# First attention stage of a two-block transformer kernel: norm after the projections, early logits, forget biases in one pass, another order of loads and turns

## The reference

```python
def rmsnorm(x, g):
    xf = x.astype(jnp.float32)
    y = xf * lax.rsqrt(jnp.mean(xf * xf, axis=-1, keepdims=True) + RMS_EPS)
    return (y * g.astype(jnp.float32)).astype(x.dtype)

def fox_attention(q, k, v, log_f):
    c = jnp.cumsum(log_f, axis=-1)
    ...
        sc = (jnp.einsum('bhqd,bhkd->bhqk', qb, k, preferred_element_type=jnp.float32) * scale
              + cb[..., :, None] - c[..., None, :])
        p = masked_softmax(sc, kpos[None, :] <= qpos[:, None])
        return jnp.einsum('bhqk,bhkd->bhqd', p.astype(v.dtype), v)

def even_mixer(h, w_in, b_f, ...):
    (fq, fk, fv, f_logit, nq, kc, vc, ks, vs, kw, vw, g_logit) = jnp.split(h @ w_in, EVEN_SPLIT_IDX, axis=-1)
    log_f = jax.nn.log_sigmoid(f_logit.astype(jnp.float32) + b_f.astype(jnp.float32)).transpose(0, 2, 1)
    o_fox = fox_attention(to_heads(fq, H_FOX), to_heads(fk, H_FOX), to_heads(fv, H_FOX), log_f)
    ...
```

## Time and profile before

| | us |
|---|---|
| median of 3 runs | 2014.54 |
| lowest, highest | 2012.95, 2021.45 |
| span of the profiled execution | 2011.9 |
| busy in it: PE, PEld, DVE, ACT, POOL | 1953.4, 1727.1, 1340.9, 1010.4, 320.4 |

### The profile page before, as it was taken

How to read it: one execution, slowest core, us unless ns; L and a number is a source line. 1 busy time by engine, 2 the same in 40 slices (tenths; PEclk the granted TensorE clock), 3 DMA queues, 4 the chain that set the end, 5 groups by cost and what they waited for, 6 DMA issues and landing times.

```text
span 2011.9 us, 34435 instructions
## 1 busy us (share of the span) xinstructions
PE 1953.4 (97%) x12338; PEld 1727.1 (86%) x12338; DVE 1340.9 (67%) x2732; ACT 1010.4 (50%) x1640; POOL 320.4 (16%) x138
## 2 busy tenths in 40 slices
PE   7998999999999999999999999999999999999998
PEld 6776787778778888999899999999999998888886
DVE  6357556656655558889787689933667766666666
ACT  5436546555554456666444455665444443333333
POOL 0000000000000000000000057877666600000000
PEclk9899999999989999999999999999999999999999
DMA  6242465533345553444343535555444455555554
GB/s 229 74 157 78 157 205 167 178 121 128 118 137 188 187 188 126 147 138 136 105 126 126 179 126 168 180 175 167 137 142 142 137 164 188 192 193 192 193 193 156
DMA packets 85150, 313.99 MB, mean 156 GB/s; under 512 B 9456, under 2 KB 9456, under 8 KB 84592
## 3 DMA queue, kind: packets, MB, share of 16 engines
q1 hardware_dynamic: 85040, 312.49, 46.6%
HBM read 311.40 MB, written 1.05 MB: 155 GB/s over the span
## 4 chain that ended last, share of the span: by engine, by line
issue 61%; PE 32%; POOL 6%; DVE 0%; POOLq 0%; DVEq 0%; ACT 0%
PE ps L414 17%; PE ps L282 12%; POOL wsplit L266 6%; PE ps L2642 3%; PE ps L430 0%; DVE work L2772 0%; DVE sq L2679 0%; POOLq L265 0%; PE ps L2718 0%; POOLq L2505 0%; DVE sq L2675 0%; DVE picks L2595 0%; PE ps L2608 0%; DVEq L2930 0%; DVE work L2687 0%
## 5 line engine op out<-in xcount | busy, mean ns | idle before, releaser
L260 ACT ACTIVATE wsplit<-ring 128x1024 fp32r<-128x1024 f32 x572 | 603.8, 1057 | 475.4 <-PE ps L414 270.4
L266 DVE TENSOR_TENSOR wsplit<-ring,wsplit 128x1024 fp32r<-128x1024 f32 x438 | 534.6, 1223 | 326.1 <-ACT wsplit L260 324.7
L282 PE MATMUL ps<-hsplit,wsplit 128*128 128x256 f32 x5064 | 646.2, 287 | 6.5 <-DVE hsplit L698 2.1
L282 PEld LDWEIGHTS ps<-hsplit,wsplit 128*128 128x128 f32 x5064 | 620.3, 193 | 14.3 <-issue 5.2
L266 POOL TENSOR_TENSOR wsplit<-ring,wsplit 128x1024 fp32r<-128x1024 f32 x134 | 320.2, 2396 | 1295.5 <-ACT wsplit L260 1295.5
L414 PE MATMUL ps<-wsplit,gsplit 128*128 128x512 f32 x1992 | 458.1, 391 | 0.0
L414 PEld LDWEIGHTS ps<-wsplit,gsplit 128*128 128x128 f32 x1992 | 374.4, 188 | 81.9 <-issue 4.2
L401 PE MATMUL ps<-wsplit,hsplit 128*128 128x512 f32 x1248 | 310.0, 406 | 17.2 <-DVE wsplit L266 10.6
L401 PEld LDWEIGHTS ps<-wsplit,hsplit 128*128 128x128 f32 x1248 | 241.9, 196 | 70.4 <-issue 18.9
L1783 PE MATMUL ps<-hsplit,wsplit 128*128 128x256 f32 x936 | 128.5, 289 | 0.0
L1783 PEld LDWEIGHTS ps<-hsplit,wsplit 128*128 128x128 f32 x936 | 116.3, 191 | 0.0
(11 more groups left out here) (318 smaller groups left out, 1698.5 us busy)
## 6 DMA issues: line engine op xcount, KB each, us to landing
ring<-in_weights SPq DMA_DIRECT2D x580, 512.0 KB, 3.3
work<-in_tables SPq DMA_DIRECT2D x1, 2123.0 KB, 12.5
xT<-in_x SPq DMA_DIRECT2D x1, 1024.0 KB, 4.9
work<-in_subkeys SPq DMA_DIRECT2D x1, 1024.0 KB, 15.2
work<-in_decay SPq DMA_DIRECT2D x2, 512.0 KB, 4.1
out_x<-work SPq DMA_DIRECT2D x2, 512.0 KB, 2.6
work<-in_w SPq DMA_DIRECT2D x1, 512.0 KB, 5.9
ring<-in_gain_row SPq DMA_DIRECT2D x1, 512.0 KB, 3.8
```

What stands on the lines that cost most here:

```text
L260: act.activation(wsplit[:, n % RING, 0, :], slab(s), ACT.Copy).then_inc(S("split", "lead"), 1)
L266: eng.tensor_tensor(wsplit[:, n % RING, 1, :], slab(s), wsplit[:, n % RING, 0, :], ALU.subtract).then_inc(S("split", RESTS[stream][0]), 1)
L282: mm = pe.matmul(dst, wsplit[:, n, a, c * P:(c + 1) * P], hsplit[:, b, c, :], start=(c == 0 and t == 0), stop=(c == KC - 1 and t == 2))
```

## The change

- **Norm.** `hT`, L385 and the second split (m0) are gone. Queries and keys are projected from the n0 split, and `rinv` is multiplied in when they are copied out of PSUM: one DVE operation of 128x512 for each turn (`fox_query_key_vector`) in place of two ACT copies. The fox and nsa values are scaled by token when they are copied out; for nsa, `rinv` is put into its own cosine and sine tables once.
- **Logits.** Forget and gate weights are one group of 56 columns, multiplied by the gains once (DVE, 128x448). `logits_tensor` runs them straight from `xT` after the second quarter of the values, 16 matmuls, each k twice: to PSUM partitions 0 to 63 and 64 to 127. The gate logits are turned by two small transposes.
- **Sum of squares.** GpSimd adds the eight chunks of squares down to two (`fold_gpsimd`, three operations of 128x512); TensorE then needs two matmuls, not eight.
- **Biases.** The running sum has its rows in four copies in each half of the partitions. It is split into a leading and a low part (one-pass type), and the bias matmul has 64 rows of the one-pass type (L824). The key side is made for each turn, two DVE operations. A turn's four score matmuls come first, then its four bias matmuls.
- **Turns.** Queries of odd and even turns have banks of their own, so a query waits for the copy of two turns before. TensorE turns the probabilities of turn u-1 ahead of the scores of u, and makes the values of u-1 after the key of u+1. ACT takes one slab lead before and one after the turned copy.
- **Loads.** Gains first, x in halves, two slabs, `small`, the third slab, the first 1940 of 4248 columns of tables. Masks and subkeys are loaded behind the nsa slabs, the other tables in the first feed-forward.
- The semaphores of the HGRN and Hyena stages are merged (`in`, `staged`), with the same instructions around them.

```diff
     def fox_tensor(pe, st, pre):
         for q in range(4):
             mm = split_columns(pe, st, q, q, 4, pre=pre)
-            if q == 0:
-                norm_tensor(pe, pre, 7)
-            if q == 2:
-                column_tensor(pe, pre, 7)
+            if q == 1:
+                logits_tensor(pe, st)
+                folded_norm_tensor(pe, 7)
         mm.then_inc(S("pair", "v"), 1)
...
         fox_query_tensor(pe, 0)
+        column_tensor(pe, pre, 7)
         fox_key_tensor(pe, 0)
-        gate_logits_tensor(pe, st)
         pe.wait_ge(S("load", "made"), 3)
+        gate_turn_tensor(pe, st)
         pe.wait_ge(S("pair", "v_sb"), 1)
         for u in range(4):
             if u < 3:
                 fox_query_tensor(pe, u + 1)
+            if u:
+                fox_probs_tensor(pe, u - 1)
             pe.wait_ge(*pair("qk_sb", u))
-            pe.wait_ge(S(st, "bias_steps"), 2 + min(u, 1))
+            pe.wait_ge(S(st, "bias_steps"), u + 3)
...
             scores_tensor(pe, qk_turn[:, 0, :], qk_turn[:, 1, :], 3, u).then_inc(S("pair", "scores"), 1)
             if u < 3:
                 fox_key_tensor(pe, u + 1)
             if u:
-                fox_probs_tensor(pe, u - 1)
                 fox_values_tensor(pe, u - 1)
...
+    def logits_tensor(pe, st):
...
+        for k in range(KC):
+            for hh in range(2):
+                mm = pe.matmul(ps[HD * hh:HD * hh + HD, 6, 0:T], strided(small_("wfg"), k * N_WFG, [[1, HD]]), xT[:, k, :],
+                               start=(k == 0), stop=(k == KC - 1))
...
+    def fox_query_key_vector(v, u):
+        v.wait_ge(*pair("qk", u))
+        v.tensor_tensor(qk_turn[:, :, :], ps[:, u % 2, :].rearrange("p (a t) -> p a t", a=2), rr[:, :, :],
+                        ALU.mult).then_inc(S("pair", "qk_sb"), 1)
...
+        if bias is not None:
+            for hh in range(2):
+                for tt, c0, keys in SEGS:
+                    h_ = slice(HD * hh, HD * hh + HD)
+                    mm = pe.matmul(ps[:, bank0 + hh, c0:c0 + keys], bias_q[h_, tt * P:(tt + 1) * P],
+                                   bias_k(bias, hh)[:, 0:keys], start=False, stop=True, skip_group_check=True)
...
-        load(xT[:, :, :], x, "x")
+        load(gains_sb[:, :], gains, "gains")
+        for half in range(2):
+            load(xT[:, 4 * half:4 * half + 4, :], x[:, 4 * half:4 * half + 4, :], f"x{half}")
+        load_slab(0, weights[0])
+        load_slab(1, weights[1])
         load(sm, small, "small")
...
```

More of the change, by code:

```diff
@@ L124, in end, with build @@
         assert self.i is None or self.n == self.per + self.base, (self.n, self.per)
-def build(nc, weights, small, tables, masks, w3, decay, subkeys, gain_row, x, out):
+def build(nc, weights, small, gains, tables, masks, w3, decay, subkeys, gain_row, x, out):
     ctx = ExitStack()
@@ L2808, in stream @@
                 load_slab(s, weights[s])
-        load(xT[:, :, :], x, "x")
-        load(sm, small, "small")
-        for s in range(RING):
-            load_slab(s, weights[s])
-        load(tab, tables, "tables")
-        load(level_masks, masks, "late")
-        load(sub, subkeys, "late")
+        load(gains_sb[:, :], gains, "gains")
+        for half in range(2):
+            load(xT[:, 4 * half:4 * half + 4, :], x[:, 4 * half:4 * half + 4, :], f"x{half}")
+        load_slab(0, weights[0])
+        load_slab(1, weights[1])
+        load(sm, small, "small")
+        load_slab(2, weights[2])
+        load(tab[:, 0:FIRST_TABLES], tables[:, 0:FIRST_TABLES], "tables")
         at = RING
@@ L2834, in _ @@
                         at += 1
+                    load(level_masks, masks, "late")
+                    load(sub, subkeys, "late")
                     continue
@@ L2879, in _ @@
         act.preload_act_table(ACT.Sqrt)
-        act.wait_ge(S("load", "made"), 2)
+        act.wait_ge(S("load", "made"), 1)
+        act.wait_ge(S("load", "gains"), 16)
         fox_scalar(act, "fox")
@@ L3115, in pack @@
     return {
-        "weights": weights, "small": small, "tables": tables, "masks": masks,
+        "weights": weights, "small": small, "gains": gs.reshape(11, KC, P).transpose(2, 0, 1).reshape(P, -1), "tables": tables, "masks": masks,
         "w3": f("filt_w3_2")[0], "decay": f("filt_decay_2"),
```

254 lines of the change are left out of this document (137 added, 117 removed).

## The result

| | before | after |
|---|---|---|
| median, us | 2013.98 (4 runs) | 1991.7 (4 runs, 1990.87 to 1992.53) |
| span of the profiled execution | 2011.9 | 1989.1 |
| first matmul | 10.59 | 10.95 |
| first scores | 44.36 | 42.57 |
| first projection of nsa | 89.41 | 67.64 |

The ratio is 0.9881, 95% interval 0.9864 to 0.9897. Forecast were 1995.7 us and a range of 1990.5 to 2005.0. A reader should know that the kernel before scatters: beside the later experiments it took 2012.46 to 2022.2 us, with granted clocks of 0.979 to 0.988, while the changed kernel stayed within 1.7 us. The trace of before that the prediction was read from is one of its best executions.

What follows compares the result with a forecast made beforehand. TensorE, busy 97% of the span, was taken as the bound. Front 2.5, turns 17.0 and behind them 0.8 sum to 20.3 us; one clock fall leaves 18.8, so 2014.5 - 18.8 = 1995.7 us, range 1990.5 to 2005.

Steps and rivals of the forecast that it cites:

- the added wait: Front: TensorE, done with key and gates at 36.1, waits 2.7 us for DVE's rest of slab 6.
- one fall of the clock: Behind the added wait: the clock falls once, costing 1.5 us (a projection 4.63 instead of 3.13).
- The start: First lead no longer waits for `small`, 430 KB less ahead, worth 1.1 us; TensorE starts at about 9.5.
- The front's sizes: First 24 matmuls 5.3 plus 2.9 us; sixteen logits matmuls 4.6 us, with 3.7 and 7.4 kept as bounds.
- A turn's scores: Each turn: scores 0.92 us (from nsa's row without biases) plus four biases 0.7, so 1.6 (1.4 to 3.0).
- The turns' projections: From first scores to nsa: five projections at 3.13 us each, 15.7 in all.
- my 28.1: TensorE's time from first scores to nsa, one wait included, against 45.05 before: 17.0 us won.
- The one wait: Turn 3, which has no query: probabilities of turn 2 come late by 1.1 us.
- My cross-check: The turns' 17.0 us won, split: scores 10.6, clock 3.0, waits 2.3, the rest the last turn's slow clock.
- Behind the turns: From nsa on: 0.8 us more won by clock; masks and subkeys delay no slab before 180 us.
- Better than that: Rival: no fall of the clock, logits pairs at 3.7, scores at 1.4; 22.0 us won, 1992.5 us; chance 0.10.
- bound by the chain of engines: Rival: turns wait for probabilities or moved transfers interfere; 6 us go, 12.8 won, 2001.7 us; chance 0.13 (chain or transfers).

Runs made afterwards that it cites:

- Experiment 7: Kernel after with slab 0 loaded between the two halves of x; 1989.13 us, ratio 0.9853.
- experiment 12: Kernel after with the logits' two halves one behind the other (eight chunks to partitions 0 to 63, then eight to 64 to 127); 1996.51 us.
- experiment 3: Kernel after with each bias matmul right behind its score matmul, still one-pass with 64 rows; 1992.68 us.
- experiment 4: Kernel after with the bias matmuls in full precision f32, 64 rows kept; 1995.46 us.
- Experiment 10: Kernel after with TensorE's old order in the turns: probabilities of turn u-1 turned behind the key of u+1; 1997.04 us, ratio 0.9903.
- experiment 6: Kernel after with masks and subkeys loaded ahead of the last nsa slab; 1992.26 us, ratio 0.9868.
- experiment 1: Kernel before without the sixteen bias matmuls of the four turns; 1995.94 us, ratio 0.9885.
- experiment 2: Kernel before with a turn's four score matmuls first and its four bias matmuls (full precision, 16 rows) behind them; 2000.29 us.
- experiment 8: Kernel after with slab 6's rest ahead of the column, masks and subkeys ahead of the last nsa slab, slab 0 between x's halves; 1988.83 us.
- experiment 11: Kernel after without GpSimd's additions of the squares: eight matmuls with ones in place of two; 1994.22 us.
- experiment 5: Kernel after with DVE's rest of slab 6 put ahead of the copy of the column; 1990.61 us, ratio 0.9858.

## Why the prediction was right and wrong

The direction and the mechanism held: the gain is in the turns, TensorE stayed the bound behind them, the added wait stood where I put it (2.85 us, forecast 2.7, at 38.04), with one fall of the clock behind it (1.5 us forecast, 4.60 - 3.1 measured). The size was short by 4.0 us of span. Along the trace, after was ahead of the forecast by 3.9 us at nsa's first projection, 3.5 at its third, 1.7 at L667, 2.5 at 1632 us and 4.0 at the end. So the error lies ahead of nsa, 3.0 us of it in the turns; a loss and a gain behind them nearly cancel, and the last 1.5 us are luck as far as the runs show. By my steps:

- **The start: wrong sign.** Forecast 9.5, measured 10.95. I counted bytes ahead of the lead, but the first ACT step waited for x until 6.09 and the lead for slab 0 until 8.54, behind the second half of x. Experiment 7 shows 9.35 with slab 0 ahead of it. That is not the whole cause: before, slab 0 lay behind all of x and `small` and was there for its lead at 8.18. From 2 to 4 us the queue moved 299 GB/s then and 206 in after; why was not tried (the 44 KB of gains now go first). Cost 1.45 us in this trace.
- **The front's sizes.** The first 24 matmuls took 7.3 us, not 8.2. The logits took 3.67 and not 4.6: the lower bound, full overlap, was the right end (experiment 12: 6.31 without). With the start these cancel: first scores at 42.57, forecast 43.4 with the clock counted. The 7.3 us are partly luck, since the same 24 matmuls took 7.0 to 8.5 in the eight kernels with this order of loads.
- **A turn's scores: the step that failed.** I took 1.6 us (bounds 1.4 to 3.0), 0.92 for the four scores and 0.7 for the four biases; it is 1.05, 2.2 us less in four turns and below my lower bound. The scores take 0.68 us up to the start of the biases, because the 0.92 of my row is a duration up to the modelled end of the last one. The biases take 0.37 up to the next projection. My lower bound of 0.5 priced all four at 256 columns, but two have 128 (one behind the other, at a projection's price, that would be 0.38), and the two halves of the rows run side by side: the single records of after show the biases starting in pairs, at 43.249 and 43.262 us, then at 43.449 and 43.465. I had used this overlap for the scores, whose row contains it, and not for the biases; how much is due to the columns and how much to the overlap is not shown. Experiments 3 and 4 size it: 0.5 us a turn for alternation, 0.56 for the type.
- **The turns' projections.** I summed durations (five of 3.13); starts lie closer, 14.9 us for five and not 15.7, since one row's end overlaps the next row's start. Together with the scores this is the 3.0 us between my 28.1 and 25.07. The one wait was right (1.1 forecast, 1.17 measured).
- **What won them.** My cross-check gave 10.6 us to the scores, 3.0 to the clock and 2.3 to the waits. By the runs the grouping alone is 12.0 of the 20.0 us (7.2 in the eight matmuls, most of the rest in the clock), 64 rows in two halves 3.0 (four turns of 0.75), the one-pass type 2.4, and some 2.5 are left for the order of turns, the queries' own banks and the copies on DVE together, which fits 3.45 us of waits becoming 1.17. These last shares are differences between single executions of unlike kernels, an estimate. Experiment 10 gives TensorE's order 5.2, but with a mismatch of its own.
- **Behind the turns: wrong.** I wrote that the masks and subkeys delay no slab before 180 us. TensorE waited 1.02 us at 171.84, and experiment 6 takes this wait away. Of 22.3 us at the third nsa projection, 20.5 are left at L667. The first two nsa projections gave 0.5 us from start to start (0.8 by their durations), forecast 0.8.
- **The second block: not forecast, and not shown to be the change's.** 1.5 us come at its last part. The product behind HGRN ran there at a granted clock of 0.96 before (46.6 us from 1653.41) and at 1.00 after, with seven more matmuls begun in the same time. Experiments 1 and 2 show 0.96 too, which looks like something that another part of the change mends. But of the eleven kernels with the change two also show 0.96 there and take the 1.5 us longer, experiments 8 and 11. First experiment 8, then after:

```profile
1629.15:1675.73 46.58, 46.58 (x198) 37.88 (x199) 30.65 (x52) 16.97 (x16) 0.00 (x0) 0.96 0.56 180
```

```profile
1632.12:1678.70 46.58, 46.58 (x205) 38.06 (x206) 31.42 (x53) 18.04 (x17) 0.00 (x0) 1.00 0.56 184
```

So a single execution of the changed kernel has this fall of the clock or has it not; whether the change makes it rarer (two of eleven, against three of three) stays open. Without these 1.5 us the profiled span would have been 2.5 us under the forecast and not 4.0.

Of the rivals none came as told. "Better than that" was nearest (1992.5) but wanted the clock not to fall; it fell as counted, and the gain came from the scores and the projections of the turns instead. The turns were not bound by the chain of engines in after; in experiments 5 and 8, which shorten the front, they became so.

The Trainium skill, page "TensorE: Matmul & The Clock Gate", section "HAM oscillation — how this bites in real kernels", has the clock fall at waits between bursts. The traces agree in part: it fell behind the wait of 2.85 us in after and behind 1.66 us in experiment 8, but not behind 1.65 us in experiment 5, nor behind the same 2.85 us in experiment 3 (in the seven other kernels with that wait it fell each time, 4.43 to 4.61 us for the projection); and before it fell at 59.62 with no wait over 0.9 us, where grouping the scores kept it up (experiment 2) with the same waits. In the one execution of each, matmuls that alternate between 64 and 16 rows did more to the clock of the turns than the waits: without the alternation (experiments 1 and 2) it stayed at full speed.

## What to carry to other kernels

Price small matmuls by how neighbours in the list relate, not one by one: put those of one shape and type together, and let neighbours use different halves of the rows or of the output partitions. When a front gets shorter, look at once at the slowest follower's queue (here DVE's) and move what nobody needs yet behind the first thing that is now waited for; otherwise the time comes back as a wait two steps on, with a fall of the clock on top. Order the first loads by first use in pieces, since half of x ahead of the first weights cost some 1.1 us here. And size an edit by the stage that it touches, not by the span of one execution.

## What the runs showed of the hardware that I had not expected

- Scores and biases alternating between 64 and 16 rows cost 4.16 us for eight full-precision matmuls, the same eight grouped 2.36 us, and the granted clock of the turns went from 0.87 to 1.00 with the grouping.
- Sixteen matmuls of 64 output columns take 3.67 us when they alternate between the halves of the output partitions and 6.31 us when they do not.
- While GpSimd adds (13.26 to 18.1 us), DVE's operations with two SBUF inputs take about twice as long: 2.31 us and not 1.23, 3.73 and not 1.67. GpSimd took 1.5 us for each 128x512, where I had reckoned 1.2. The Trainium skill, page "GPSIMD Engine Reference", section "1. Specifications", says that its SBUF interface is shared with VectorE, with contention when VectorE reads two SBUF inputs; the trace agrees.
- The same instructions, from L667 to the product behind HGRN, took 1444.6 to 1448.6 us in eleven kernels, and the part behind it 357.0 or 358.5, with granted clocks of 1.00 or 0.96 over its first 46.6 us.
